# First stage of a conditioned decoder layer: modulation columns in two halves, first products block by block

## The chip, the cores and the metric

The kernel runs on one core of one Trainium2 chip. The metric is the device time of one execution in microseconds (us), the median of several; lower is better. Columns of a matmul are counted along its moving operand; a bank is one of the eight 128 x 512 float32 pieces of PSUM.

## The reference

`x` is (1, 1024, 1024) float32, `c` is (1, 1024). The stage that the change touches computes this (cut to it):

```python
mod = silu(c) @ w_ada + b_ada                  # w_ada: (1024, 6*1024)
sh1, sc1, gt1, sh2, sc2, gt2 = split(mod, 6)
h = rmsnorm(x, norm1_g) * (1 + sc1) + sh1      # (1024, 1024)
proj = h @ w_in                                # (1024, 3600): gq, gk, gv, gg, ga, hq, hf, hi, hg
a_logit = ga @ gla_w_a2 + gla_b_a              # ga has rank 16
```

Behind it come six units of chunked gated linear attention (two GLA pairs of heads, four HGRN2 heads), the output projection with its gated residual, a second modulated norm, a mixture of 32 experts with routing to two of them, and a final modulated norm.

## The kernel before

All work is laid out by hand: five engines, each with its own written order, tied by semaphores. The names in the order and trace rows are those of tiles, and a line of a helper serves all its callers.

**The first stage.** `h` is needed transposed (model dimension on partitions, tokens along the free dimension), as eight inner blocks k of 128 by 1024 tokens, and split in a high part `HT` and a low part `HL` (`HFULL` is the unrounded value and lies at the address of `HL`), since each float32 product is made of three float32r matmuls (`product`, L1945 to L1947: high x high, low x high, high x low). Its steps are:

- SP (the DMA queue of SyncE) loads tokens 0 to 511 of x (two DMAs of 1 MB), then sixteen slices of `w_ada` into `AST`, 512 KB each (eight for the scale `sc1`, eight for the shift `sh1`), then the first of the four weight chunks `WF`, the other half of x, and the other chunks. A chunk is 128 columns of `w_in`, 512 KB.
- ScalarE (ACT) squares x to sums (`square`, L808), takes the root and scales the rows (L815); VectorE does the inverse (`inverse`) and scales the second half's rows (L1288).
- VectorE accumulates `acc += slice * c_act[k]` for sixteen slices of 1024 columns (`add_slice`, L1242 and L1244) into `ACC` (scale) and `ACCB` (shift).
- TensorE (PE) transposes x block by block (`x_transposes`, L1929, four 128 x 128 transposes per block and token half), and sums each accumulator over partitions by `col_job` (L1910): eight matmuls with one moving column, whose stationary operand is 128 columns of the accumulator. Between the two jobs stand two matmuls whose result nobody reads (L1936). VectorE turns the sums into the columns `GS1` and `SH1` (`column`, L1258, L1260).
- Per block, ACT evacuates the transposes with scale and bias to `HT` (`x_evac`, L841), and VectorE makes the low part in two steps (`x_low`, L1320 from PSUM, then L1324).
- TensorE then runs `k_jobs(0)`, one job after the other and each over all eight blocks: query and key of token half 0, the rank-16 gate `ga`, query, key and gate of half 1, then `a`. The blocks of half 1 are transposed between these jobs.

**What follows.** VectorE's order goes on behind the last `x_low` with the small constants, the low parts of the value chunks (`low`, L1309, behind ACT's L822), eight slices for the next row (`unit_slice`, L1242 and L1244, out of the two buffers `AR`, which GpSimd (POOL) refills each time one has been used), and then the decay steps of unit 0 (L1390 onward), on which ACT's exponentials (L850) and the evacuation of value job 1 (L908) wait. TensorE goes on with the value jobs (`gv`), the row job and the jobs of unit 1.

Of the kernel before, what the change touches and what calls it, by code (L numbers as in the profile page):

```python
# [27 lines left out]
F32 = mybir.dt.float32  # L28
# [20 lines left out]
def layer_kernel(nc, x, c, w_ada, b_ada, norm1_g, w_in, gla_w_a2, gla_b_a, gla_norm_g, hg_norm_g,  # L49
# [113 lines left out]
    X_BANK = [2, 3, 4, 5, 6, 1, 2, 3, 4, 5, 6, 7, 2, 3, 4, 5]  # L163
    X_AHEAD = 6
# [28 lines left out]
    with ExitStack() as ctx:  # L193
# [38 lines left out]
        AST = at("AST", 96, [P, 8, D])  # L232
# [153 lines left out]
        COL = [PS[:, b * HALF:b * HALF + KD] for b in (7, 0)]  # L386
# [28 lines left out]
        c_in = sem("c_in")  # L415
# [11 lines left out]
        slab_in = [sem(f"slab_in{i}") for i in range(8)]  # L427
        ar_in = [sem(f"ar_in{i}") for i in range(2)]
        ar_used = sem("ar_used")
        ast_used = sem("ast_used")  # L430
        w_raw = [sem(f"w_raw{i}") for i in range(WSLOTS)]
# [17 lines left out]
        rr_h = sem("rr_h")  # L449
# [4 lines left out]
        xt_done = sem("xt_done")  # L454
# [67 lines left out]
        yg_in = [sem(f"yg_in{t}") for t in range(NT)]  # L522
# [8 lines left out]
        win = w_in.rearrange("a (p k) n -> p (a k) n", k=KD)  # L531
# [3 lines left out]
        def ada_slice(v, k):  # L535
            src, col = ADA[v]
            return ada_w[src][:, k, col:col + D]
# [8 lines left out]
        def _(sp):  # L546
# [3 lines left out]
            def load_early(v):  # L550
                for k in range(KD):
                    n = EARLY.index(v) * KD + k
                    if n >= 8:
                        sp.wait_ge(ast_used, n - 7)
                    sp.dma_start(AST[:, n % 8, :], ada_slice(v, k)).then_inc(slab_in[n % 8], 16)

# [6 lines left out]
            load_early("sc1")  # L563
            load_early("sh1")
            load_chunk(0)
            for g in range(2, NT // 2):
                load_x(g)
            for n in range(1, WSLOTS):
                load_chunk(n)
            last_use = {}  # L570
            for u in range(UNITS):
                for name in ("q", "k", "f"):
                    if (u, name) in chunk_at:
                        last_use[chunk_at[(u, name)]] = number[(u, name, 1)]
# [73 lines left out]
            for t in range(NT):  # L648
                sp.dma_start(YG[t][:, :, :], ys_rows[:, 0:3:2, t, :]).then_inc(yg_in[t], 16)
# [8 lines left out]
        def _(pool):  # L658
# [11 lines left out]
            pool.wait_ge(ast_used, KD + 4)  # L670
            with nc.allow_non_contiguous_dma(reason="short vectors"):
# [9 lines left out]
                pool.dma_start(GCOL[:, 2, :], norm_f_g.rearrange("(p k) -> p k", k=KD)).then_inc(later_in, 16)  # L681
            n = 0
# [105 lines left out]
        def _(act):  # L788
            A = nc.scalar.activation
            act.dma_start(C8[:], col_view(c)).then_inc(c_in, 16)  # L790
            act.wait_ge(c_in, 16)
# [1560 lines left out]
```

## Time and profile before

| | |
|---|---|
| median of 3 runs | 1070.38 us (1068.85 to 1071.96) |
| the profiled execution | 1076.19 us, span 1074.4 us |
| TensorE busy | 991.8 us (92%) |
| VectorE busy | 797.4 us (74%) |
| ScalarE busy | 527.6 us (49%) |
| granted TensorE clock, mean | 0.969 |

The profile is one execution, 0.5% above the median of the runs; its span is 1.8 us shorter than its own time. Busy shares are means over stages with different limits. What happens in the first 110 us is read from the timeline, the chain of waits and the stretches between two instants.

### The profile page before, as it was taken

The numbers are of one execution on the slowest core, as the hardware profiler recorded it, in microseconds if no ns is written. First come the engines' busy times: TensorE is split into PE (matmuls) and PEld (weight loads), VectorE is DVE, ScalarE is ACT, GpSimd is POOL, SyncE is SP. The second block draws the span as 40 slices with busy tenths as digits, with TensorE's granted clock in tenths as the row PEclk, the third lists the DMA queues.
The fourth block names the chain that finished last, engine by engine and source line by source line (L and its number), as shares of the span: only waits on it lengthen the run. The fifth ranks groups of instructions, "written<-read, shape, count | busy, mean of one in ns | idle before, by whom it ended". The sixth has DMA issues, their size and how long they took to land.

```text
span 1074.4 us, 15416 instructions
## 1 busy us (share of the span) xinstructions
PE 991.8 (92%) x5654; PEld 780.0 (73%) x5654; DVE 797.4 (74%) x1476; ACT 527.6 (49%) x921; POOL 118.7 (11%) x151
## 2 busy tenths in 40 slices
PE   2899988999898999999989899789999999999996
PEld 3669778987896998989978688456666666666642
DVE  7768668944992886958677755868888887878828
ACT  4454332653265465555562321265666666565532
POOL 0200001000100000000010000023122112222200
PEclk9798989999998999999989899999999999999998
DMA  9733433330323224130292122789999999999285
GB/s 363 231 98 98 137 99 99 99 98 23 116 80 99 79 76 141 60 99 1 83 402 51 79 80 101 286 295 341 370 374 372 361 366 367 350 353 359 96 304 212
DMA packets 79881, 206.78 MB, mean 192 GB/s; under 512 B 11750, under 2 KB 40502, under 8 KB 71628
## 3 DMA queue, kind: packets, MB, share of 16 engines
q1 hardware_dynamic: 58080, 156.25, 40.2%
q0 software_dynamic: 15120, 43.72, 12.5%
q10 hardware_dynamic: 6620, 6.00, 1.8%
q8 instruction: 39, 0.64, 0.3%
q14 instruction: 22, 0.18, 0.1%
HBM read 189.61 MB, written 24.71 MB: 199 GB/s over the span
## 4 chain that ended last, share of the span: by engine, by line
PE 56%; DVE 22%; DMA 13%; issue 4%; ACT 4%; SPq 0%; ACTq 0%; DVEq 0%; POOLq 0%
PE PS L1945 10%; PE PS L1947 10%; PE PS L1946 10%; DMA WGU<-in_w_exp_up 7%; PE PS L2216 4%; PE PS L2010 3%; DMA AR<-in_w_ada 3%; DVE ACC L1244 3%; DVE AT L1418 3%; PE PS L2224 3%; PE PS L2222 3%; PE PS L2223 3%; DVE WL L1309 2%; PE PS L2207 2%; PE PS L2326 1%
## 5 line engine op out<-in xcount | busy, mean ns | idle before, releaser
L1945 PE MATMUL PS<-WH,HT 128*128 128x256 f32 x512 | 148.9, 291 | 3.9 <-ACT GVB L908 2.2
L1946 PE MATMUL PS<-WL,HT 128*128 128x256 f32 x512 | 146.8, 287 | 0.0
L1947 PE MATMUL PS<-WH,HL 128*128 128x256 f32 x512 | 146.8, 287 | 0.0
L1782 DVE TENSOR_TENSOR WGL<-WGU,WGH 128x1024 fp32r<-128x1024 f32 x96 | 116.9, 1219 | 20.0 <-ACT WGH L1152 18.8
L1418 DVE COPY_PREDICATED AT<-MASK,PS 128x64 f32<-128x64 uint8 x320 | 72.9, 228 | 68.7 <-PE PS L2021 50.2
L1152 ACT ACTIVATE WGH<-WGU 128x1024 fp32r<-128x1024 f32 x96 | 98.6, 1062 | 43.6 <-DMA WGU<-in_w_exp_up 32.6
L1945 PEld LDWEIGHTS PS<-WH,HT 128*128 128x128 f32 x512 | 100.4, 196 | 7.0 <-issue 7.0
L1946 PEld LDWEIGHTS PS<-WL,HT 128*128 128x128 f32 x512 | 100.2, 196 | 0.0
L1947 PEld LDWEIGHTS PS<-WH,HL 128*128 128x128 f32 x512 | 100.2, 196 | 0.0
L2222 PE MATMUL PS<-WGH,XGTH 128*96 128x512 f32 x192 | 88.6, 461 | 0.0
L1820 DVE TENSOR_TENSOR WDL<-WDN,WDH 128x2048 fp32r<-128x2048 f32 x32 | 73.4, 2292 | 16.8 <-ACT WDH L1162 16.8
L1945 PE MATMUL PS<-HT,WH 128*128 128x512 f32 x192 | 79.7, 415 | 3.3 <-DVE HL L1324 2.5
L1000 ACT ACTIVATE O<-PS 128x128 f32<-128x128 f32 x64 | 17.5, 274 | 125.6 <-PE PS L2059 97.7
L1947 PE MATMUL PS<-HT,WL 128*128 128x512 f32 x192 | 76.6, 399 | 0.0
L1946 PE MATMUL PS<-HL,WH 128*128 128x512 f32 x192 | 76.5, 398 | 0.0
L2224 PE MATMUL PS<-WGH,XGTL 128*96 128x512 f32 x192 | 76.0, 396 | 0.0
L2223 PE MATMUL PS<-WGL,XGTH 128*96 128x512 f32 x192 | 75.3, 392 | 0.0
L1244 DVE SCALAR_TENSOR_TENSOR ACC<-AR,CA,ACC 128x1024 f32<-128x1024 f32 x42 | 53.9, 1284 | 27.8 <-DMA AR<-in_w_ada 18.3
L730 POOL DMA_INDIRECT XG<-xn_rows,IDXG x32 | 38.7, 1209 | 307.3 <-DVE YB L1795 112.9
L2216 PE MATMUL PS<-WGU,XGTF 128*96 128x512 f32 x128 | 61.7, 605 | 0.0
L1162 ACT ACTIVATE WDH<-WDN 128x2048 fp32r<-128x2048 f32 x32 | 61.3, 1917 | 0.0
L1140 ACT ACTIVATE XGTH<-PS 128x384 fp32r<-128x384 f32 x32 | 15.7, 490 | 78.9 <-PE PS L2207 78.9
(347 smaller groups left out, 2268.6 us busy)
## 6 DMA issues: line engine op xcount, KB each, us to landing
WGU<-in_w_exp_gate SPq DMA_DIRECT2D x32, 1024.0 KB, 12.4
WGU<-in_w_exp_up SPq DMA_DIRECT2D x32, 1024.0 KB, 18.4
WDN<-in_w_exp_down SPq DMA_DIRECT2D x32, 1024.0 KB, 13.8
AR<-in_w_ada POOLq DMA_DIRECT2D x32, 512.0 KB, 4.0
WF<-in_w_in SPq DMA_DIRECT2D x28, 512.0 KB, 5.6
AST<-in_w_ada SPq DMA_DIRECT2D x16, 512.0 KB, 8.7
AR<-in_w_ada_final POOLq DMA_DIRECT2D x16, 512.0 KB, 4.7
YG<-expert_rows SPq DMA_DIRECT2D x8, 1024.0 KB, 12.5
```

Source lines behind the costliest of these rows:

```text
L1152: A(WGH[(NCH * s + part) % 4][:], WGU[s][:, :, KC * part:KC * part + KC, :], ACT.Copy).then_inc(wgh_ready, 1)
L1244: i = V.scalar_tensor_tensor(out=acc, in0=w, scalar=CA[:, k:k + 1], in1=acc, op0=ALU.mult, op1=ALU.add)
L1418: link(V.copy_predicated(level(a, s)[:, :, 1, :], level(MASK[:, l, :], s)[:, :, 1, :], level(src, s)[:, :, 1, :]))
L1782: V.tensor_tensor(WGL[s][:, :, ks, :], WGU[s][:, :, ks, :], WGH[(NCH * s + c) % 4][:].bitcast(F32), ALU.subtract).then_inc(wgl_ready, 1)
L1820: V.tensor_tensor(WDL[s][:], WDN[s][:], WDH[s % 2][:].bitcast(F32), ALU.subtract)
L1945: MM(ps, wh, xh, start=first, stop=False)
L1946: MM(ps, wh, xl, start=False, stop=False)
L1947: return MM(ps, wl, xh, start=False, stop=last)
L2216: MM(ps, XGTF[:, par, k - KS, :], WGU[s][:, :, k, :], start=(k == KS), stop=False)
L2222: MM(ps, XGTH[:, par, k, :], wh, start=False, stop=False)
L2223: MM(ps, XGTH[:, par, k, :], wl, start=False, stop=False)
L2224: last = MM(ps, XGTL[:, par, k, :], wh, start=False, stop=(k == KS - 1))
```

## The change

All of x is loaded first, and its squares, roots and row scalings are done for both token halves on ACT. The slices of `w_ada` come as column halves of 256 KB (512 columns): part 0 for inner blocks 0 to 3, part 1 for blocks 4 to 7; sixteen slots, 32 slices. The inner dimension is now blocked contiguously (`w_in` as `(k p)`, x as `k * P:(k + 1) * P`), before it was strided (`k::KD`). The bias and gain vectors come in by rows and are transposed on TensorE. Query and key products of unit 0 run block by block into four banks of their own (`FIRST`): four blocks for both token halves, then, behind the sums of part 1, the other four. Four of the shift slices of part 1 are not accumulated on VectorE, but multiplied on TensorE (`shift_slices`). `x_evac` writes both `HT` and `HFULL`, so that `x_low` is one subtraction. Seven unread matmuls take the place of two.

```diff
     def k_jobs(u):
         if is_gla(u):
             if u == 0:
-                return [("q", 0), ("k", 0), ("ga", 0), ("q", 1), ("k", 1), ("ga", 1), ("a", 0), ("a", 1)]
+                return [("ga", 0), ("ga", 1), ("a", 0), ("a", 1)]
...
-    X_BANK = [2, 3, 4, 5, 6, 1, 2, 3, 4, 5, 6, 7, 2, 3, 4, 5]
-    X_AHEAD = 6
+    PARTS = 2
+    KP = KD // PARTS
+    x_order = [(g, k) for part in range(PARTS) for g in range(2) for k in range(KP * part, KP * part + KP)]
+    X_BANK = [4, 5, 6, 7] + [(4, 5, 6)[i % 3] for i in range(12)]
+    early_order = [(v, part, k) for part in range(PARTS) for k in range(KD) for v in range(2)]
+    AST_SLOTS = 16
+    SHIFT_ON_PE = [(1, 1, k) for k in range(KD // 2, KD)]
+    early_on_dve = [e for e in early_order if e not in SHIFT_ON_PE]
+    first_products = [("q", 0), ("k", 0), ("q", 1), ("k", 1)]
...
-            load_early("sc1")
-            load_early("sh1")
-            load_chunk(0)
             for g in range(2, NT // 2):
                 load_x(g)
-            for n in range(1, WSLOTS):
+            load_early(0)
+            load_chunk(0)
+            load_chunk(1)
+            load_early(1)
+            for n in range(2, WSLOTS):
                 load_chunk(n)
...
+            def x_evac(i):
+                g, k = x_order[i]
+                act.wait_ge(xb_ready, i + 1)
+                gs, dst = GS1[:, k:k + 1], slice(g * HALF, (g + 1) * HALF)
+                A(HT[:, k, dst], XB[i], ACT.Identity, scale=gs, bias=SH1[:, k:k + 1])
+                A(HFULL[:, k, dst], XB[i], ACT.Identity, scale=gs, bias=SH1[:, k:k + 1]).then_inc(xh_ready, 1)
...
+            act.wait_ge(mod1_ready, 1)
+            for i in range(8):
+                x_evac(i)
...
+            act.wait_ge(mod1_ready, 2)
+            for i in range(8, 14):
+                x_evac(i)
+            first_evac("q", 0)
+            x_evac(14)
+            first_evac("k", 0)
+            x_evac(15)
...
             scale_rows(0)
+            early_slices(0, 6)
             scale_rows(1)
+            early_slices(6, 16)
+            bias_columns()
+            columns(0)
+            lows(0, k_chunks(0))
+            for i in range(8):
+                x_low(i)
+                early_slices(16 + i, 17 + i)
+            early_slices(24, len(early_on_dve))
+            columns(1)
+            for i in range(8, 16):
+                x_low(i)
...
+            def shift_slices():
+                for i, e in enumerate(SHIFT_ON_PE):
+                    n = early_order.index(e)
+                    pe.wait_ge(slab_in[n % AST_SLOTS], 16 * (n // AST_SLOTS + 1))
+                    for b in range(KP):
+                        last = MM(SUM_SH[1][:, b, 1 + i:2 + i], AST[:, n % AST_SLOTS, b * P:(b + 1) * P], CA[:, e[2]:e[2] + 1],
+                                  start=True, stop=True)
+                last.then_inc(shift_ready, 1)
...
+            for i in range(4):
+                x_transposes(i)
+            pe.wait_ge(small_in, 64)
+            TR(BIAS, BROW[:, :], IDENT[0:3 * KD, 0:3 * KD]).then_inc(col_ready, 1)
+            unread(4)
+            early_sums(0)
+            unread(3)
+            for i in range(8):
+                first_block(i)
+                if i != 3:
+                    x_transposes(i + 4 if i < 3 else i + 3)
+            pe.wait_ge(ca_ready, 1)
+            shift_slices()
+            early_sums(1)
+            for i in range(8, 16):
+                first_block(i)
+                if i + 3 < 16:
+                    x_transposes(i + 3)
+            for name, half in k_jobs(0):
                 k_job(0, name, half)
```

The order that results on TensorE, from its first instruction to the second block of products (`PS<-XR,IDENT` are the unread matmuls, `PS<-ONESF,ACC` the sums over partitions). Before:

```order
L1929 MATMUL PS<-IDENT,XR 128x128 x24
L1910 MATMUL PS<-ONESF,ACC 128x1 x8
L1936 MATMUL PS<-XR,IDENT 128x512 x2
L1910 MATMUL PS<-ONESF,ACCB 128x1 x8
L1945 MATMUL PS<-HT,WH 128x512
L1946 MATMUL PS<-HL,WH 128x512
L1947 MATMUL PS<-HT,WL 128x512
```

With the change:

```order
L1971 MATMUL PS<-IDENT,XR 128x128 x16
L2109 MATMUL PS<-IDENT,BROW 128x24
L1956 MATMUL PS<-XR,IDENT 128x512 x4
L1942 MATMUL PS<-ONESF,ACC 128x1 x4
L1942 MATMUL PS<-ONESF,ACCB 128x1 x4
L1956 MATMUL PS<-XR,IDENT 128x512 x3
L1991 MATMUL PS<-HT,WH 128x512
L1992 MATMUL PS<-HL,WH 128x512
L1993 MATMUL PS<-HT,WL 128x512
```

Ahead of the first product eight transposes and eight sums less are issued, and five unread matmuls and one small transpose more.

TensorE between the eighth and the ninth block of products, with the change (the last rows of block 7, the transposes of block 10, the shift slices, the sums of part 1, the first rows of block 8):

```order
L1991 MATMUL PS<-HT,WH 128x512
L1992 MATMUL PS<-HL,WH 128x512
L1993 MATMUL PS<-HT,WL 128x512
L1971 MATMUL PS<-IDENT,XR 128x128 x4
L1950 MATMUL PS<-CA,AST 128x1 x16
L1942 MATMUL PS<-ONESF,ACC 128x1 x4
L1942 MATMUL PS<-ONESF,ACCB 128x1 x4
L1991 MATMUL PS<-HT,WH 128x512
L1992 MATMUL PS<-HL,WH 128x512
L1993 MATMUL PS<-HT,WL 128x512
```

Before, nothing of this stood between products: twenty-four matmuls of one moving column now do.

VectorE from the first column sums to the second block. Before:

```order
L1258 TENSOR_TENSOR GS_134<-PS,BCOL 128x8
L1260 SCALAR_TENSOR_TENSOR GS_134<-GS_134,GCOL 128x8
L1309 TENSOR_TENSOR WL<-WF,WH 128x1024
L1258 TENSOR_TENSOR SH_135<-PS,BCOL 128x8
L1320 SCALAR_TENSOR_TENSOR HFULL<-PS,GS_134,HT 128x512
L1324 TENSOR_SCALAR HL<-HFULL,SH_135 128x512
L1320 SCALAR_TENSOR_TENSOR HFULL<-PS,GS_134,HT 128x512
L1324 TENSOR_SCALAR HL<-HFULL,SH_135 128x512
```

With the change:

```order
L1280 COPY BCOL<-PS 128x16
L1281 COPY GCOL<-PS 128x8
L1287 TENSOR_TENSOR GS_135<-PS,BCOL 128x4
L1288 SCALAR_TENSOR_TENSOR GS_135<-GS_135,GCOL 128x4
L1290 TENSOR_TENSOR SH_136<-PS,BCOL 128x4
L1344 TENSOR_TENSOR WL<-WF,WH 128x1024 x2
L1354 TENSOR_TENSOR HL<-HFULL,HT 128x512
L1264 TENSOR_SCALAR ACC<-AST,CA 128x512
L1354 TENSOR_TENSOR HL<-HFULL,HT 128x512
L1264 TENSOR_SCALAR ACCB<-AST,CA 128x512
```

Both low parts of the query and key weights now stand ahead of the first low part of x, and behind each of the first eight low parts stands one half slice of part 1.

## Rows read from the trace of the kernel before

**Rows 1.** the page: busy us of each engine, share of the span, instructions

```profile
PE 991.8 (92%) x5654; PEld 780.0 (73%) x5654; DVE 797.4 (74%) x1476; ACT 527.6 (49%) x921; POOL 118.7 (11%) x151
```

**Rows 2.** chain of waits, 60 to 103 us: start us, us, what

```profile
64.78 0.49 DVE HL L1324
...
69.52 0.68 DVE ACC L1242
...
71.80 5.87 DMA AR<-in_w_ada
...
88.35 1.30 DVE ACC L1244
...
101.88 0.36 PE PS L1945
```

**Rows 3.** timeline of PE: start us, us, line, out<-in, instructions [idle before <-releaser]

```profile
18.82 5.36 PE L1929 MATMUL PS<-IDENT,XR 128*128 128x128 f32 x24 [18.82 <-ACT XR L815]
23.97 3.78 PE L1910 MATMUL PS<-ONESF,ACC 128*128 128x1 f32 x16
27.61 3.58 PE L1936 MATMUL PS<-XR,IDENT 128*128 128x512 f32 x4
32.39 3.96 PE L1910 MATMUL PS<-ONESF,ACCB 128*128 128x1 f32 x16 [1.20 <-DVE ACCB L1244]
38.88 0.77 PE L1945 MATMUL PS<-HT,WH 128*128 128x512 f32 x1 [2.52 <-DVE HL L1324]
...
54.15 2.96 PE L1929 MATMUL PS<-IDENT,XR 128*128 128x128 f32 x24 [0.17 <-DVE XR L1288]
...
61.46 0.48 PE L1945 MATMUL PS<-HT,WH 128*128 128x512 f32 x1
...
72.45 0.39 PE L1970 MATMUL PS<-HT,WGS 128*32 128x512 f32 x1
```

**Rows 4.** stretches: from:to, us, busy us (instructions) by engine, granted clock, DMA share, GB/s

```profile
10.00:20.00 10.00, 1.18 (x6) 1.21 (x7) 9.29 (x14) 7.12 (x10) 0.00 (x0) 1.00 1.04 396
...
27.60:31.20 3.60, 3.59 (x5) 1.17 (x5) 3.49 (x4) 0.00 (x0) 3.60 (x6) 0.54 1.10 353
...
38.90:44.50 5.60, 5.60 (x17) 4.66 (x18) 5.42 (x10) 3.62 (x6) 0.00 (x0) 0.50 1.11 334
```

**Rows 5.** timeline of ACT, 5 to 40 us

```profile
6.17 1.06 ACT L808 ACTIVATE SQX<-XR 128x1024 f32<-128x1024 f32 x1 [2.08 <-DMA XR<-in_x]
...
7.36 1.06 ACT L808 ACTIVATE SQX<-XR 128x1024 f32<-128x1024 f32 x1
...
8.85 1.06 ACT L808 ACTIVATE SQX<-XR 128x1024 f32<-128x1024 f32 x1 [0.35 <-DMA XR<-in_x]
...
12.73 0.20 ACT L804 ACTIVATE RR<-TA 128x4 f32<-128x4 f32 x1
14.41 4.27 ACT L815 ACTIVATE XR<-XR,RR 128x1024 f32<-128x1024 f32 x4 [1.47 <-DVE RR L1233]
31.63 1.06 ACT L822 ACTIVATE WH<-WF 128x1024 fp32r<-128x1024 f32 x1 [12.95 <-DMA WF<-in_w_in]
36.65 4.12 ACT L841 ACTIVATE HT<-PS,SH,GS 128x512 fp32r<-128x512 f32 x6 [3.96 <-DVEq L1335]
```

**Rows 6.** timeline of PE, warm unread matmuls at the end of the program

```profile
1023.03 6.17 PE L2308 MATMUL PS<-X,IDENT 128*128 128x512 f32 x14
```

**Rows 7.** timeline of DVE: slices, a column step, a weight chunk's low part

```profile
23.13 9.21 DVE L1244 SCALAR_TENSOR_TENSOR ACCB<-AST,CA,ACCB 128x1024 f32<-128x1024 f32 x7
32.37 0.17 DVE L1258 TENSOR_TENSOR GS<-PS,BCOL 128x8 f32<-128x8 f32 x1
...
32.88 1.23 DVE L1309 TENSOR_TENSOR WL<-WF,WH 128x1024 fp32r<-128x1024 f32 x1
```

**Rows 8.** line L1320 alone: instructions, ns min/median/max, first and last start

```profile
L1320 DVE SCALAR_TENSOR_TENSOR HFULL<-PS,GS,HT x16: 744/746/751, 37.5 to 64.0; 128x512 f32<-128x512 f32 x16
```

**Rows 9.** timeline of PE: transposes whose stationary columns are adjacent, at full clock

```profile
220.26 1.23 PE L2046 MATMUL PS<-IDENT,O 128*128 128x128 f32 x8 [0.25 <-ACT GVB L908]
```

More of the change, by code:

```diff
@@ L426, in layer_kernel @@
         br_in = sem("br_in")
-        slab_in = [sem(f"slab_in{i}") for i in range(8)]
+        slab_in = [sem(f"slab_in{i}") for i in range(AST_SLOTS)]
         ar_in = [sem(f"ar_in{i}") for i in range(2)]
@@ L548, in load_x, with load_early @@
                 sp.dma_start(XR[:, 2 * g:2 * g + 2, :], x_rows[:, 2 * g:2 * g + 2, :]).then_inc(x_in[g], 16)
[L550 to L555, printed above, removed]
+            def load_early(part):
+                for n, (v, p, k) in enumerate(early_order):
+                    if p == part:
+                        if n >= AST_SLOTS:
+                            sp.wait_ge(ast_used, n - AST_SLOTS + 1)
+                        sp.dma_start(AST[:, n % AST_SLOTS, :], ada_slice(EARLY[v], k, part * HALF, HALF)).then_inc(
+                            slab_in[n % AST_SLOTS], 16)
             def load_chunk(n):
@@ L808, in square @@
                 chain(A(SQX[:], XR[:, t, :], ACT.Square, accum_out=SS[:, t:t + 1]))
-            for t in range(4):
-                square(t)
-            root_of(0, 4, D).then_inc(rr_ready, 1)
-            act.wait_ge(inv_ready, 1)
-            for t in range(4):
-                A(XR[:, t, :], XR[:, t, :], ACT.Copy, scale=RR[:, t:t + 1]).then_inc(xr_ready, 1)
+            for g in range(2):
+                for t in range(4 * g, 4 * g + 4):
+                    square(t)
+                root_of(4 * g, 4 * g + 4, D).then_inc(rr_ready, 1)
+            for g in range(2):
+                act.wait_ge(inv_ready, g + 1)
+                for t in range(4 * g, 4 * g + 4):
+                    A(XR[:, t, :], XR[:, t, :], ACT.Copy, scale=RR[:, t:t + 1]).then_inc(xr_ready, 1)
             act.wait_ge(table_zero, 16)
@@ L826, in highs @@
                     high(u, name)
-            high(0, "q")
+            highs(0, k_chunks(0))
             def evac(job):
@@ L833, in evac, with first_evac @@
                 return pj_free[n % 2]
[L835 to L842 removed]
+            def x_evac(i):
[4 more added lines that the diff above has]
+                A(HFULL[:, k, dst], XB[i], ACT.Identity, scale=gs, bias=SH1[:, k:k + 1]).then_inc(xh_ready, 1)
+            def first_evac(name, half):
+                n = first_products.index((name, half))
+                act.wait_ge(first_ready, n + 1)
+                A((Q if name == "q" else K)[:, 0, half * HALF:(half + 1) * HALF], FIRST[(name, half)], ACT.Copy,
+                  scale=float(P // 2) ** -0.5 if name == "q" else 1.0).then_inc(first_free, 1)
             def item(u, i):
@@ L959, in _ @@
             highs(0, v_chunks(0))
-            for name, half in k_jobs(0)[3:]:
+            first_evac("q", 1)
+            first_evac("k", 1)
+            for name, half in k_jobs(0):
                 k_evac(0, name, half)
@@ L1964, in k_job @@
                 for k in range(KD):
-                    if (u, name) == (0, "q"):
-                        pe.wait_ge(xl_ready, half * KD + k + 1)
-                        if half == 0 and k == 2:
-                            x_transposes(0, range(X_AHEAD, KD))
                     if name == "ga":
```

177 lines of the change are left out of this document (81 added, 96 removed).

## Prediction

> **What bounds the kernel now.** The page says that TensorE is busy 92% of the span and VectorE 74% [rows 1]; that is an average, so I went on to the first 110 us. The chain of waits there [rows 2] is the view that decides: it does not run over TensorE, but from the last low part of x (VectorE, L1324, ends at 65.3 us) through the value weights to eight slices out of `AR`, of which the chain waits for the transfers (69.5 to 89.65 us), through the decay steps to the value job that starts at 101.88. So the number to forecast is when the last low part of x is ready: what it slips, everything behind it slips, since the eight slices stand behind it in VectorE's order. The timeline of TensorE [rows 3] shows the stage before it: transposes from 18.8, first product at 38.88, then nearly unbroken work. The stretches [rows 4] give the clock: 0.50 of full speed (the 1.2 GHz level) for the first 5.6 us of products, because the column sums and an idle time lay ahead of them.
>
> **How rows and instructions go together.** The written order has eight column sums where the trace has sixteen rows [rows 3], and two unread matmuls where it has four: a plain float32 matmul stands in two rows. So one column sum costs 3.78 / 8 = 0.47 us, and the second job of eight took 3.96 us, 0.49 each, with the clock partly down: its price hardly hangs on the clock. A transpose is one row.
>
> **The change, step by step.**
>
> 1. *x first.* The two MB of x landed for squares at 6.17 and 8.85 [rows 5]; at 396 GB/s [rows 4] each further MB takes 2.6 us, so the other half is there at 11.5 and 14.1 and is not waited for. A square costs 7.36 - 6.17 = 1.19 [rows 5]: four more from 12.93 end at 17.7, the root at 18.1. Four row scalings take 4.27 [rows 5], so the first transposes start at 22.4, not 18.8. The later four scalings end at 26.7, ahead of the two weight chunks. The sixteen half slices (4.2 MB) land by 24.7. The first weight chunk was there at 31.63, behind 10.5 MB [rows 5]; now the second one ends 9.4 MB, so by about 30, and ACT's two high parts (1.06 each) end by 32 and are not late.
> 2. *VectorE, part 0.* A slice of 1024 columns costs 9.21 / 7 = 1.32 [rows 7]; I take half, 0.66, for 512 columns (upper bound 0.75, a 512-column operation of this kind from PSUM [rows 8]). Sixteen and the two inverses end at 26.6. TensorE is later than that, so VectorE is not the bound.
> 3. *TensorE up to the sums.* 16 transposes at 5.36 / 24 = 0.22 [rows 3] end at 26.0, the bias transpose at 26.2. Four unread matmuls: two took 3.58 [rows 3], 1.79 each at the low clock; fourteen rows took 6.17 [rows 6], 0.88 per matmul at full clock. Before, the clock came back 2.9 us into this work (mean 0.54 over 3.6 us, rows 4). So 1.6 of them at 1.79 and 2.4 at 0.88: 5.0 us, to 31.2 (bounds 29.7 and 33.4). Eight sums, 3.8: 35.0.
> 4. *To the first product.* Three column steps on VectorE at 0.2 [rows 7]: 35.6. ACT now evacuates twice, 4.12 / 6 = 0.69 each [rows 5]: 37.0. VectorE makes two weight low parts first (1.23 each, rows 7): 38.1; then one subtraction of 512 columns, half of 1.23: 38.7. First product at 38.9, where it was 38.88. Nothing is gained up to here. The three unread matmuls (2.6) lie in this wait and should keep the clock up, so I take full speed for what follows.
> 5. *Blocks 0 to 7.* 48 rows from 61.46 to 72.45 [rows 3]: 0.229 per matmul. 48 matmuls 11.0, plus 28 transposes at 2.96 / 24 = 0.123 [rows 3], 3.4: to 53.3. ACT needs 1.4 per block, VectorE 0.6 + 0.66; both keep up, and VectorE's last half slice (28th) is done at about 53.
> 6. *The stop in the middle.* Sixteen shift matmuls and eight sums, all of the form of the column sum: 24 x 0.47 = 11.3 us, to 64.6. No product can cover them, since block 8 needs what they give, and the transposes that could run ahead (three banks) have run. Before, the same eight sums of the scale lay ahead of the first product, where TensorE had nothing to do. Moving four half slices saves VectorE 4 x 0.66 = 2.6 us and costs TensorE 7.6. Then four column steps 0.8, two evacuations 1.4, a subtraction 0.6: block 8 starts at 67.4.
> 7. *Blocks 8 to 15.* The clock falls in those 14 us, as it did before behind far less; the low stretch then lasts 5.6 us [rows 4] and costs half of it, 2.8. The last x transposes stand behind block 12: 30 matmuls 6.9, 20 transposes 2.5, clock 2.8: 79.6. ACT, held up by two evacuations of finished products (0.6 each), is done with block 15 at 81.3, the last low part at 81.9. Before: 65.3. **The slip is 16.6 us.**
> 8. *Behind it.* Constants, value weights and the eight slices are the same instructions: 24.4 us from the last low part to the end of the slices [rows 2], transfers of 0.5 MB through two buffers. That they are hidden better or worse I bound by 2 us either way: 5.87 was waited in the longest case [rows 2], where two weight chunks were loading too; these now wait for the first gate job, and so fall into the slices again. TensorE is through its gate jobs at 81.9 + (6 + 32) x 0.229 = 90.6, before at 72.45 + 16 x 0.229 = 76.1 [rows 3]: 14.5 later, less than VectorE's slip, so it doesn't set more.
> 9. *At nothing.* New loads of bias rows (landed long before TensorE has done its transposes), merged semaphores, the two evacuations where ACT was idle.
>
> **Rules against rows.** The rows of the column sums stand 3.78 / 16 = 0.236 us apart [rows 3], and the sum goes by that. The Trainium skill (TensorE: Matmul & The Clock Gate, LDWEIGHTS) gives a weight load of 128 columns 107 ns; an estimate by it makes the thirty-two small matmuls cost 3.4 us, not 15.1, and the whole change +5 us.
> With adjacent stationary columns, at full clock, eight transposes took 1.23, 0.15 each with the tail [rows 9]; with columns eight apart 0.123 [rows 3]. The Trainium skill (SBUF — State Buffer, Door 1) says that accesses which cross to a new 16-byte line pay a penalty, which would speak for this change's contiguous blocks; these two rows show none.
>
> **The sum.** Made on the profiled execution: 1076.2 + 16.6 = 1092.8. That execution stands 0.5% above the median; on the median: 1070.4 + 16.6 = 1087.0.
>
> **Rivals.**
> - *The clock stays down.* If the three unread matmuls don't hold it, they take 5.4 instead of 2.6 (first product 1.7 later) and blocks 0 to 7 pay 2.8: +21, 1091.5. For it: the column sums that stand between the two unread groups lost the clock before. Against: the second group ends about 1 us ahead of the products.
> - *The small matmuls are cheap.* If each takes the pace of a transpose, 0.123 [rows 3], the thirty-two save 32 x 0.35 = 11.2: +5.4, 1075.8. For it: the one moving column is next to nothing, and a transpose loads as many stationary columns. Against: 0.47 in both jobs. The page on TensorE comes to about this time.
> - *Other side: strided reads were the cost.* All stationary operands of the sums and transposes were read eight elements apart, now they are adjacent. If that brings a small matmul to 0.12 (part 0 ends 2.8 earlier, the stop shrinks from 11.3 to 2.9) and 48 transposes to half price (2.9), and the clock outlives the short stop (2.8): 16.6 - 2.8 - 8.4 - 2.9 - 2.8 = -0.3, and 1070. From 0.12 a small matmul down it is no loss, below that a gain, to about 1067. Against it: rows 9. The page on SBUF has this rule.
> - *The change does not reach the end:* the slip is taken up behind the stage. TensorE waits little there and VectorE's chain has only transfers to give: 2 us, not 16. I see no more, but a chain is one view.
>
> **How the numbers follow.** Forecast 0.64, clock down 0.12, cheap small matmuls 0.12, other side 0.07, taken up behind 0.05. A difference under 0.3% (3.2 us) can't be told from none with this kernel. Slower: 0.64 + 0.12 + 0.12 = 0.88; the last two cases, 0.12, are half same (0.06), half faster (0.06). The forecast's own range is 1082 to 1091 (step 3's bounds, the transfers, the runs' 1.5 us). With the clock case above and the cheap one below it becomes 1075 to 1093.
>
> **What would show it.** In the changed profile: first product within 2 us of 38.9; the shift matmuls as 32 rows at 0.236 each and 16 rows of sums behind them, with no product between; clock 0.50 in the stop and for some 5 us of block 8 and on; the last `HL` at 80 to 84 us; the value job's start at about 118. Wrong if the stop is shorter than 6 us, if the first product stands before 35, or if the last `HL` slips but the value job does not.

## The result, and the profile after

The changed kernel takes 1080.75 us (median of 4 runs, 1078.54 to 1083.05) against 1069.66 for the kernel before, run beside it on the same chip (1068.85 to 1071.96): ratio 1.010, 95% interval 1.0072 to 1.0128. That is slower by 11.1 us, where 16.6 was forecast (1087.0, range 1075 to 1093). The profiled execution took 1083.05 us, with a span of 1081.2 and a mean granted clock of 0.969, as before.

On the page after, TensorE is busy 995.1 us and VectorE 787.2, before 991.8 and 797.4 [rows 1]; nothing can be read from that. The timeline of TensorE up to the second part's first product is the counterpart of [rows 3]:

```profile
22.18 3.65 PE L1971 MATMUL PS<-IDENT,XR 128*128 128x128 f32 x16 [22.18 <-ACT XR L831]
25.76 0.30 PE L2109 MATMUL PS<-IDENT,BROW 24*128 24x24 f32 x1
25.99 4.16 PE L1956 MATMUL PS<-XR,IDENT 128*128 128x512 f32 x8
29.98 0.95 PE L1942 MATMUL PS<-ONESF,ACC 128*128 128x1 f32 x8
30.79 1.03 PE L1942 MATMUL PS<-ONESF,ACCB 128*128 128x1 f32 x8
31.69 2.82 PE L1956 MATMUL PS<-XR,IDENT 128*128 128x512 f32 x6
35.64 0.50 PE L1991 MATMUL PS<-HT,WH 128*128 128x512 f32 x1 [1.13 <-DVE HL L1354]
...
49.90 3.63 PE L1950 MATMUL PS<-CA,AST 128*128 128x1 f32 x32
53.40 1.07 PE L1942 MATMUL PS<-ONESF,ACC 128*128 128x1 f32 x8
54.33 1.84 PE L1942 MATMUL PS<-ONESF,ACCB 128*128 128x1 f32 x8
59.36 0.79 PE L1991 MATMUL PS<-HT,WH 128*128 128x512 f32 x1 [3.19 <-DVE HL L1354]
```

The first product stands at 35.64, 3.2 us earlier than the 38.88 of before, and the stop in the middle is there, as 32 rows (the shift matmuls) and 16 rows (the sums), but it lasts 9.5 us from its first row to block 8, not 14.1. The stretches after (before, and the meaning of the columns: [rows 4]) show the clock: up through blocks 0 to 7, at 0.50 (1.2 GHz) from 54.3 to 64.5, the end of the stop and the first five us of block 8 and on.

```profile
36.00:50.00 14.00, 14.00 (x78) 11.64 (x76) 11.56 (x18) 7.92 (x13) 1.06 (x2) 1.00 0.71 212
50.00:54.30 4.30, 4.30 (x41) 4.30 (x40) 0.67 (x1) 0.00 (x0) 0.00 (x0) 0.99 0.53 208
54.30:64.50 10.20, 7.01 (x24) 5.95 (x24) 2.74 (x7) 5.44 (x8) 0.00 (x0) 0.50 0.00 0
```

The chain of waits after, behind the last low part of x (before: [rows 2]):

```profile
72.64 0.69 DVE HL L1354
...
80.07 7.17 DMA AR<-in_w_ada
...
99.02 1.29 DVE ACC L1266
...
112.55 0.55 PE PS L1991
```

The last low part ends at 73.3, before at 65.3: 8.1 us. The eight slices end at 100.3, before at 89.65: 10.7. The value job starts at 112.55, before at 101.88: 10.67 us. So 8.1 us are lost ahead of that low part and 2.6 behind it. That these 10.7 reach the end rests on the medians, which differ by 11.1. The two traces agree with it only in part: the last head output (`OTS`) is evacuated 9.3 us later (538.4 against 529.1), but the spans differ by 6.8. Of the difference 3.5 us stand in one place, where the first gather of the experts' rows waits 8.0 us behind the last store of `XN` in the trace of before and 4.5 in the one after; over all the traces of this case that wait lies between 4.4 and 8.1, and none of the edits touches it.

### The profile page after: what moved, and what is told of

It is laid out like the page before. It is cut to its first block, busy times and chain, and to the rows that moved or that the text cites. A ratio compares the mean times of both kernels' runs of the same rounds, so it can differ in the third digit from the quotient of the medians.

```text
span 1081.2 us, 15575 instructions
## 1 busy us (share of the span) xinstructions
PE 995.1 (92%) x5697; PEld 781.7 (72%) x5697; DVE 787.2 (73%) x1474; ACT 542.0 (50%) x941; POOL 108.5 (10%) x151
## 4 chain that ended last, share of the span: by engine, by line
PE 60%; DVE 19%; DMA 11%; ACT 5%; issue 4%; ACTq 0%; SPq 0%; DVEq 0%; POOLq 0%
PE PS L1991 11%; PE PS L1993 10%; PE PS L1992 10%; DMA WGU<-in_w_exp_up 7%; PE PS L2272 4%; PE PS L2053 3%; PE PS L2280 3%; PE PS L2278 3%; PE PS L2279 3%; DVE AT L1448 3%; DMA AR<-in_w_ada 3%; DVE ACC L1266 2%; DVE WL L1344 2%; PE PS L2263 1%; PE PS L2382 1%
## 5 line engine op out<-in xcount | busy, mean ns | idle before, releaser
L1991 PEld LDWEIGHTS PS<-WH,HT 128*128 128x128 f32 x512 | 100.4, 196 | 11.3 <-issue 11.3
L1992 PEld LDWEIGHTS PS<-WL,HT 128*128 128x128 f32 x512 | 100.3, 196 | 0.0
```

Source lines behind the costliest of these rows:

```text
L1991: MM(ps, wh, xh, start=first, stop=False)
L1992: MM(ps, wh, xl, start=False, stop=False)
```

## The experiments

Each run has beside it runs of the kernel before on the same chip; ratios are to those. Each was traced once. "FD" is VectorE's step behind the eight slices (100.34 us in the changed kernel), the last landmark of the stage that stands in all of these kernels.

**Stride put back.** The sums and shift matmuls read their stationary columns four elements apart; the sums then belong to other columns of the model dimension than the rest of the kernel takes them for, and nothing else differs.

```diff
-   last = MM(dst, acc[:, lo:lo + P], ONESF[:, 0:1], ...)
+   last = MM(dst, acc[:, part * HALF + b:(part + 1) * HALF:KP], ONESF[:, 0:1], ...)
...
-   ... AST[:, n % AST_SLOTS, b * P:(b + 1) * P], CA[:, e[2]:e[2] + 1],
+   ... AST[:, n % AST_SLOTS, b::KP], CA[:, e[2]:e[2] + 1],
```

> The changed kernel, but the stationary columns of its column sums and shift matmuls lie four elements apart (the sums then belong to other columns; nothing else is altered). In the changed kernel such a matmul took 0.22 us (two rows 0.108 apart) where I had forecast 0.47 from the kernel before. Theory A (the clock made the difference): they still take 0.22 at full clock, the 24 in the middle about 6 us, last HL at 73 us, time as the changed kernel, 1081. Theory B (adjacent columns made it): 0.4 to 0.47 each, the middle 10 to 11 us, first product 1 to 2 us later, last HL at 78 to 81, time 1086 to 1088.

One run, 1083.91 us (before on that chip: 1069.95). Timeline of TensorE, this experiment:

```profile
29.84 1.80 PE L1942 MATMUL PS<-ONESF,ACC 128*128 128x1 f32 x8
31.49 2.00 PE L1942 MATMUL PS<-ONESF,ACCB 128*128 128x1 f32 x8
...
51.88 7.52 PE L1950 MATMUL PS<-CA,AST 128*128 128x1 f32 x32
59.27 2.00 PE L1942 MATMUL PS<-ONESF,ACC 128*128 128x1 f32 x8
61.13 2.00 PE L1942 MATMUL PS<-ONESF,ACCB 128*128 128x1 f32 x8
66.33 0.79 PE L1991 MATMUL PS<-HT,WH 128*128 128x512 f32 x1 [3.19 <-DVE HL L1354]
```

The same instructions at the same places take twice as long: 32 shift rows 7.5 us and not 3.6, the first two groups of sums 1.65 and 1.87 us from start to start and not 0.81 and 0.90. The stop is 14.5 us, and with it the forecast's stop comes out nearly to the number (14.1). The first two groups are the clean comparison, since the granted clock is 1.00 there in both kernels; in the stop it fell at 54.0, among the shift rows, and they kept their distance of 0.23 us. Two stretches of this experiment:

```profile
30.00:32.00 2.00, 2.00 (x11) 2.00 (x10) 0.00 (x0) 0.00 (x0) 1.69 (x3) 1.00 1.13 279
...
56.00:58.00 2.00, 2.00 (x10) 2.00 (x10) 0.00 (x0) 0.00 (x0) 0.00 (x0) 0.50 0.00 0
```

The weight loads of these rows (line of the first group's sums alone: ns min/median/max), first this experiment, then the changed kernel:

```profile
L1942 PEld LDWEIGHTS PS<-ONESF,ACC x16: 307/329/329, 29.4 to 60.9; 128*128 128x128 f32 x16
```

```profile
L1942 PEld LDWEIGHTS PS<-ONESF,ACC x16: 190/192/232, 29.6 to 54.1; 128*128 128x128 f32 x16
```

What follows: the price of a small matmul is set by how its stationary columns are read, 0.41 to 0.47 us when they are strided and 0.22 when adjacent, at full clock. That is theory B. The last low part starts at 79.4 (72.6 in the changed kernel) and the landmark `FD` at 106.1, 5.8 us later. The one time, 1083.9, is only 3.2 above the changed kernel's median and below theory B's 1086 to 1088. The 6.6 us by which the first head output is late in this trace (236.1 against 229.5) are 5.1 at the last one, so I take the size from the landmarks of the stage.

**Contiguous blocks in the kernel before.** Only the layout and the bias rows, nothing split.

```diff
-   win = w_in.rearrange("a (p k) n -> p (a k) n", k=KD)
+   win = w_in.rearrange("a (k p) n -> p (a k) n", p=P)
...
-   last = MM(ps[:, k:k + 1], acc[:, k::KD], ONESF[:, 0:1], ...)
+   last = MM(ps[:, k:k + 1], acc[:, k * P:(k + 1) * P], ONESF[:, 0:1], ...)
...
-   last = TR(XB[i][:, t * P:(t + 1) * P], XR[:, 4 * g + t, k::KD], IDENT[:])
+   last = TR(XB[i][:, t * P:(t + 1) * P], XR[:, 4 * g + t, k * P:(k + 1) * P], IDENT[:])
```

> The kernel before, with nothing of the change but the contiguous inner blocks (w_in, x and accumulators by k * P:(k + 1) * P, bias and gain by rows and one small transpose). Theory A (stride costs nothing, the clock does all): sums as before, 3.96 us, 1069.7 as before. Theory B (stride costs half of a small matmul): the second job of eight sums 1.8 to 2.2 us instead of 3.96, first product at 36.7 to 37.1, then the same 5.6 us at half clock, time 1067.5.

1070.3 us against 1069.95, ratio 1.000 (0.9983 to 1.0017). Its TensorE timeline:

```profile
25.42 1.95 PE L1916 MATMUL PS<-ONESF,ACC 128*128 128x1 f32 x16
27.23 1.96 PE L1944 MATMUL PS<-XR,IDENT 128*128 128x512 f32 x4
33.53 3.57 PE L1916 MATMUL PS<-ONESF,ACCB 128*128 128x1 f32 x16 [4.33 <-DVE ACCB L1247]
39.62 0.76 PE L1953 MATMUL PS<-HT,WH 128*128 128x512 f32 x1 [2.53 <-DVE HL L1327]
```

The first job fell from 3.78 [rows 3] to 1.95: theory B as to the price. The second did not, and the rest of theory B missed: TensorE, done sooner, then waited 4.33 us for VectorE, the clock went to 0.50, and sixteen rows took 3.57 us at 1.2 GHz. So adjacent columns cost 0.11 us a row at the upper level and 0.21 at the lower; strided ones cost 0.21 to 0.24 at either (last experiment ahead of block 0 and in its stop, and [rows 3]). A faster engine waited longer, lost its clock and gave the gain back.

A second thing hides in this comparison. The whole stage starts later here: `c` landed about 1.2 us later, VectorE's first row is at 5.28 and not at 4.12, and its last early slice ends 1.1 us later. So the first product at 39.62 against 38.88 is 0.4 us early if counted from VectorE's start. In all twelve other traces that row is at 5.06 to 5.59; of the kernel before there is one trace, so whether the other layout of the small loads does this, or that one execution was early, is open.

**The same with three unread matmuls behind the second job.**

```diff
    col_job("sh1", ACCB, ast_used, 2 * KD)
+   pe.wait_ge(mod1_ready, 1)
+   for _ in range(3):
+       MM(PS[:, 7 * HALF:8 * HALF], IDENT[:], XR[:, 0, 0:HALF], start=True, stop=True)
```

> As b_contig, and three unread matmuls behind the second job of column sums (2.6 us at full clock, inside the wait for the first low part). Theory A (the clock is held as in the changed kernel): the first products at full clock, first product at 37, the 2.8 us of the half-speed stretch gone as well, time 1064.5 to 1065.5. Theory B (the clock falls anyway, or the unread ones delay the first product): as b_contig or slower by up to 2.

1070.94 us, ratio 1.0003 (0.9985 to 1.002). Theory B. The clock had fallen before the second job, and work behind it comes too late:

```profile
33.49 3.57 PE L1916 MATMUL PS<-ONESF,ACCB 128*128 128x1 f32 x16 [3.88 <-DVE ACCB L1247]
36.92 5.30 PE L1948 MATMUL PS<-XR,IDENT 128*128 128x512 f32 x6
41.40 1.05 PE L1956 MATMUL PS<-HT,WH 128*128 128x512 f32 x1
```

**Nothing of the shift on TensorE** (the changed kernel, VectorE makes those four half slices itself).

```diff
-   SHIFT_ON_PE = [(1, 1, k) for k in range(KD // 2, KD)]
+   SHIFT_ON_PE = []
```

> The changed kernel, but all four shift slices are accumulated on VectorE (SHIFT_ON_PE empty). TensorE loses 32 rows (3.5 us) in the middle; VectorE's last half slice ends at 50.7 + 4 x 0.78 = 53.8 instead of 50.7, and TensorE waits for it from 49.9. Theory A (the stop is set by TensorE's small matmuls): sums 2 us at full clock, stop 2 us or more shorter, 1079. Theory B (the stop is a chain over three engines, and what TensorE sheds VectorE takes on): sums end at 53.8 + 2.7 = 56.5 against 56.2, time within 1 us of 1081.

1077.9 us, ratio 1.0061 (1.0042 to 1.0081). TensorE in the stop:

```profile
53.56 1.02 PE L1940 MATMUL PS<-ONESF,ACC 128*128 128x1 f32 x8 [3.12 <-DVE ACC L1266]
...
59.17 0.79 PE L1988 MATMUL PS<-HT,WH 128*128 128x512 f32 x1 [2.98 <-DVE HL L1352]
```

The 3.5 us that TensorE sheds it waits for VectorE; block 8 is where it was (59.17 against 59.36), `FD` at 99.35. The sums end at 56.2, which is theory B. The median is 2.9 us lower than the changed kernel's (by the ratios, 1.0061 against 1.010, it is about 4), of which the landmarks show 1.0. In the traces another 2.6 lie between the first and the last head output: 306.3 us here, 308.9 in the changed kernel. That stretch holds the same work in all kernels and takes 306.1 to 309.1 over all the traces, so I don't count it to the edit.

**The split taken back** (all slices, shift matmuls and both groups of sums ahead of block 0).

```diff
    early_sums(0)
-   unread(3)
-   ...
    pe.wait_ge(ca_ready, 1)
    shift_slices()
    early_sums(1)
+   unread(3)
+   for i in range(8):
+       first_block(i)
...
-   early_slices(6, 16)
+   early_slices(6, len(early_on_dve))
```

> The changed kernel with the split taken back: VectorE makes all slices before the first product, the shift matmuls and both groups of sums stand ahead of block 0, and the sixteen blocks follow without a stop. VectorE's part-0 slices end at 28.0 us in the changed kernel and twelve more at 0.785 us would end at 37.5; then 48 small rows at 0.11 (about 5 us, or twice that at the low clock), and the first product at 42 to 45, 7 to 9 us later than the changed kernel's 35.64. Theory A (the stop costs what TensorE stands without products in it, 9.5 us from 49.9 to 59.36, and the low clock behind it some 2.5 us more, so the split gives back more than it won): the last low part of x at 68 to 71 instead of 73.3, and 1075 to 1079. Theory B (the total work ahead of block 15 is the same and only its place changes): last low part within 1 us of 73.3, and 1080 to 1082. If it comes out over 1083, the split was worth having.

1084.11 us, ratio 1.0132 (1.011 to 1.0154): over 1083, so neither theory, and the third case. Its TensorE:

```profile
38.12 6.96 PE L1946 MATMUL PS<-CA,AST 128*128 128x1 f32 x32 [7.00 <-DMA AST<-in_w_ada]
44.94 1.84 PE L1938 MATMUL PS<-ONESF,ACC 128*128 128x1 f32 x8
46.65 1.84 PE L1938 MATMUL PS<-ONESF,ACCB 128*128 128x1 f32 x8
48.35 4.85 PE L1952 MATMUL PS<-XR,IDENT 128*128 128x512 f32 x6
53.64 0.50 PE L1987 MATMUL PS<-HT,WH 128*128 128x512 f32 x1 [0.43 <-DVE HL L1354]
```

I had priced VectorE's slices (end of the last: 37.5 expected, 42.2 measured) and not the slabs' transfers: TensorE waits 7.0 us for a slab, and does the next 14 us of work at the lower level. The first product is at 53.6, the last low part ends at 79.4. With x first and half slices, the split does gain something (`FD` at 100.3, here 105.1), so it is the frame around it that loses. Which part of the frame (x first, the half slices, the second evacuation, products block by block) loses how much, no run separates.

**The two late weight chunks earlier.**

```diff
-   sp.wait_ge(pj_ready, last_use[before] + 1)
+   if before < 2:
+       sp.wait_ge(first_ready, 4)
+   else:
+       sp.wait_ge(pj_ready, last_use[before] + 1)
```

> The changed kernel, where SyncE waits for four of the first product's blocks instead of the first gate job ahead of the two late weight chunks (their slots are free by then), so these 2.1 MB move before the eight slices of VectorE and not beside them. The changed kernel's slices took 22.6 us from their first row to the decay steps (77.70 to 100.3), the kernel before 20.2, with 7.17 and 5.87 us of waiting for one transfer. Theory A (the chunks beside the slices cost them their transfers): 20 us or less for the slices and 1077.5 to 1079. Theory B (the slices are bound by their own 4.2 MB through two buffers, whatever moves beside them): 22 to 23 us and 1080 to 1082.

1077.1 us, ratio 1.0064 (1.0041 to 1.0087). VectorE's timeline, the first slice and the step behind the eighth, this experiment and then the changed kernel:

```profile
77.64 0.75 DVE L1267 TENSOR_SCALAR ACC<-AR,CA 128x1024 f32<-128x1024 f32 x1
...
97.00 1.23 DVE L1423 TENSOR_TENSOR FD<-FD,GVB 128x1024 f32<-128x1024 f32 x1
```

```profile
77.70 0.75 DVE L1264 TENSOR_SCALAR ACC<-AR,CA 128x1024 f32<-128x1024 f32 x1
...
100.34 1.22 DVE L1420 TENSOR_TENSOR FD<-FD,GVB 128x1024 f32<-128x1024 f32 x1
```

19.4 us for the slices, not 22.6: theory A. The median moved by 3.7. Two things are to be set right in what I had expected. The two chunks are 1.05 MB together, not 2.1. And the semaphore counts finished products and not blocks, so they are issued at 75.2 and not at 79.0, 2.4 us ahead of the first slice where they were 1.3 behind it; that was enough to get them mostly out of the way.

The size is less certain than the two rows make it look. With the chunks issued behind the first slice the eight slices took 21.0 to 22.6 us (six traces, mean 21.6), with both issued ahead of it 19.4 here and 21.0 in the three mends below. In the kernel before, where one goes ahead and one falls among them, they took 20.2. So the chunks cost up to 3.3 us, about 1.4 on the mean.

**Two unread matmuls fewer** (`unread(4)` becomes `unread(2)` ahead of the first sums).

> The changed kernel with two unread matmuls ahead of the first sums instead of four. VectorE's half slices end at 28.03 us, the sums start at 29.98 behind the unread ones. Theory A (the unread ones only delay the sums, 0.88 us each at full clock, once the clock is up): sums at 28.2, first product at 33.9 instead of 35.64, the stop 1.7 earlier, and 1078.5 to 1079.5. Theory B (with fewer of them the clock falls again ahead of the first product): a first product at 34 to 35 at the low clock, 2.8 us lost behind it, and 1080.5 to 1082.

1078.27 us, ratio 1.0078 (1.0054 to 1.0102). TensorE:

```profile
33.97 0.50 PE L1991 MATMUL PS<-HT,WH 128*128 128x512 f32 x1 [1.13 <-DVE HL L1354]
...
48.24 4.55 PE L1950 MATMUL PS<-CA,AST 128*128 128x1 f32 x32
52.65 1.84 PE L1942 MATMUL PS<-ONESF,ACC 128*128 128x1 f32 x8
...
59.40 0.79 PE L1991 MATMUL PS<-HT,WH 128*128 128x512 f32 x1 [3.19 <-DVE HL L1354]
```

The first product is 1.7 us earlier, as theory A has it, at full clock. But in this stop the clock is at 0.50 from 50.7 us on, behind some 23 of the 32 shift rows, where the changed kernel kept it until the second group of sums: rows that took 0.11 us take 0.21, and block 8 starts at 59.40 as before. The 1.7 us are gone in the stop. `FD` is at 98.68, 1.7 earlier, by slices that took 21.0 us; the last low part ends at 73.3 as before, so that gain is not the one expected.

**One unread matmul in the stop.**

```diff
    shift_slices()
+   for _ in range(2):
+       MM(PS[:, 7 * HALF + 256:8 * HALF], IDENT[:], XR[:, 0, 0:256], start=True, stop=True)
    early_sums(1)
```

> The changed kernel with one unread matmul (two of 256 columns) between the sixteen shift matmuls and the sums of the second part. In the changed kernel the clock fell at about 54.3 us, 4.4 us after the last product, and stayed at 0.50 until 64.5. Theory A (a matmul of full width in the stop keeps the clock): it costs 0.9 to 1 us of TensorE, the second job of sums stays at 1.03 us instead of 1.84, and blocks 8 to 10 run at full clock (2.5 us less): the last low part of x at 70.5 to 72 instead of 73.3, and 1078.5 to 1080. Theory B (it only delays, and the clock falls all the same): block 8 at 60.3 instead of 59.36, low clock until 65, and 1081 to 1082.5.

1081.09 us, ratio 1.011 (1.0088 to 1.0132): theory B. Its stretches:

```profile
50.00:55.00 5.00, 5.00 (x44) 4.90 (x42) 0.99 (x2) 0.00 (x0) 0.00 (x0) 0.99 0.50 193
55.00:66.00 11.00, 7.81 (x29) 6.81 (x30) 2.74 (x7) 5.23 (x8) 0.00 (x0) 0.54 0.00 0
```

The clock went down behind it all the same, at 54.9, and block 8 came at 61.07, 1.7 later; 0.35 of that stood ahead of the stop already (first shift row at 50.25 against 49.90).

**Three mends together** (two unread, no shift on TensorE, the chunks early).

> The changed kernel with three mends at once: two unread matmuls instead of four ahead of the first sums, no slices moved to TensorE, and the two late weight chunks loaded early. Alone they brought 2.5, 2.9 and 3.7 us against the changed kernel's 1080.75. Theory A (they are worth on different stretches, so they add up): 1071.5 to 1073. Theory B (first and second both end in the stop, where VectorE's slices or the clock take the gain): 1074 to 1076. In neither is it under the kernel before: the stop of TensorE in the middle stays.

1075.8 us, ratio 1.0065 (1.0044 to 1.0086): theory B, at its upper end. By ratio three mends together can't be told from the best of them alone (1.0064). In the trace the last low part ends at 71.0 (2.3 earlier, where each of the first two alone moved it by nothing: one had VectorE behind it, the other the clock) and `FD` stands at 96.4, 3.9 earlier.

**The kernel before, adjacent columns, clock held.** Six unread matmuls between the two groups of sums instead of two, and two behind them.

```diff
-   for _ in range(2):
+   for _ in range(6):
        MM(PJ[0], IDENT[:], XR[:, 0, 0:HALF], start=True, stop=True)
    col_job("sh1", ACCB, ast_used, 2 * KD)
+   pe.wait_ge(mod1_ready, 2)
+   for _ in range(2):
+       MM(PJ[0], IDENT[:], XR[:, 0, 0:HALF], start=True, stop=True)
```

> The kernel before with inner blocks in rows of their own (adjacent stationary columns, as in the changed kernel), without split, and six unread matmuls instead of two between the two groups of sums, two more between the second group and the first product. So TensorE works until about 33.2, when VectorE has the second matrix ready (33.5). Theory A (the clock is all that kept the adjacent columns from a gain): the second group of sums at full clock takes 1.9 us instead of 3.6, first product at 38.0 instead of 38.9, the first blocks at full clock (2.8 us), last low part of x at 61.5 instead of 65.3, and 1065.5 to 1068. Theory B (behind the first product VectorE and ScalarE set the pace, 16 low parts at 1.3 us and more, or the clock falls in any case): last low part at 64 to 66, and 1069 to 1071.

1068.89 us, ratio 0.9993 (0.9983 to 1.0004): theory B. TensorE:

```profile
27.06 7.09 PE L1944 MATMUL PS<-XR,IDENT 128*128 128x512 f32 x12
33.99 1.84 PE L1916 MATMUL PS<-ONESF,ACCB 128*128 128x1 f32 x16
...
38.36 0.47 PE L1956 MATMUL PS<-HT,WH 128*128 128x512 f32 x1 [0.23 <-DVE HL L1327]
39.45 0.50 PE L1956 MATMUL PS<-HT,WH 128*128 128x512 f32 x1 [0.16 <-DVE HL L1327]
```

The second job at the upper level takes 1.84, and the stretch 38.9 to 44.5 has a granted clock of 1.00 where it had 0.50 [rows 4]. Yet each of the first blocks of products now waits for VectorE's low part, and these come 1.18 us apart in both kernels. The last one ends at 64.5, before at 65.3. The 2.8 us that I had put on the clock in this stage weren't there to win.

**And VectorE relieved.** In that kernel ScalarE makes the whole value of inner blocks 2, 4 and 6, and squares two rows of x earlier.

```diff
+   FULL_ON_ACT = (2, 4, 6)
...
+   if k in FULL_ON_ACT:
+       last = A(HFULL[:, k, dst], XB[i], ACT.Identity, scale=GS1[:, k:k + 1], bias=SH1[:, k:k + 1])
...
+   if k in FULL_ON_ACT:
+       v_.sem_inc(xt_done, 1)
+       V.tensor_tensor(HL[:, k, hs], HFULL[:, k, hs], HT[:, k, hs].bitcast(F32), ALU.subtract)...
+       continue
```

> The kernel before with adjacent columns and the held clock (as in b_hold), in which VectorE set the pace of the first blocks at 1.18 us per low part. Here ScalarE makes the whole value of three of eight inner blocks, as the changed kernel does for all (VectorE then needs one subtraction of about 0.65 us), and squares two of the later four rows of x ahead of its last evacuations. Theory A (the stage before was bound by VectorE at 1.18 us a block, and by ScalarE's squares ahead of the second half of x): the second group of transposes at 51 to 52 us instead of 53.45, the last low part of x at 60.5 to 62 instead of 64.0 (64.8 in the kernel before), and 1065 to 1067. Theory B (ScalarE is then the bound, or TensorE's products are): last low part at 63 to 65, and 1068 to 1070.

1066.35 us against 1068.62, ratio 0.9979 (0.9963 to 0.9996), the only one of these kernels that is below the kernel before, by 0.2%. VectorE:

```profile
61.23 0.69 DVE L1332 TENSOR_TENSOR HL<-HFULL,HT 128x512 fp32r<-128x512 f32 x1 [1.06 <-ACT HFULL L849]
...
62.62 0.49 DVE L1338 TENSOR_SCALAR HL<-HFULL,SH 128x512 fp32r<-128x512 f32 x1
```

The last low part starts at 62.6, 2.2 us earlier than the 64.78 of [rows 2]; ScalarE is late at block 6 and gives a part of it back. The landmark lies between the two theories, and the time is in theory A's range.

## Why the prediction was right, and where its sum was wrong

The sign, the place and the shape held: the number to forecast was the last low part of x, TensorE stood without products in the middle, the clock fell there, and what was lost up to the low part went through to the end. The size didn't. Of the 16.6 us 8.1 came, and 2.6 more came from behind.

Of the signs that I had named, the numbers missed: the first product was to be within 2 us of 38.9 (35.64), the small rows 0.236 apart (0.11), the last low part at 80 to 84 (73.3), the value job at about 118 (112.55). The order of the rows, the clock in the stop and behind it, and the value job slipping with the low part held. The time is below the forecast's own range (1082 to 1091) and within the wide one only through the lower bound that I had drawn for cheap small matmuls. And it is closer to the forecast than the working deserves: 2.6 us behind the low part, which the sum had at nothing, made up for a third of what was priced too high ahead of it.

- *Step 1, x first.* Transposes from 22.18 (forecast 22.4), done at 25.76 with the bias transpose behind them. Right.
- *Step 2, VectorE.* The half slices stand 0.785 us apart, 16.04 to 16.82: worse than the upper bound I gave (0.75), and 0.66 was my value. Half the columns cost 0.6 of the time. It did no harm, since TensorE's sums came later; it would in the version without a split.
- *Step 3, up to the sums, failed twice.* The four unread matmuls (eight rows) took 4.0 us, not 5.0: only the first row was slow, 0.99 us, the other seven stood 0.43 apart. The reading behind the 5.0 was off too: a mean of 0.54 over 3.6 us [rows 4] leaves 3.3 us at the lower level and not 2.9. And the two groups of sums took 1.7, not 3.8. First product 35.64 instead of 38.9.
- *Step 4.* From the sums to the product 3.9 us forecast, 3.95 measured.
- *Step 5, blocks 0 to 7.* 14.4 forecast, 14.3 measured.
- *Step 6, the stop, failed by its price.* "24 x 0.47 = 11.3 us": it was 6.2 (49.90 to 56.1), of which the shift rows 3.5 at full clock and the sums 2.8, the second job with the clock down. The wait behind it, 2.8 forecast, was 3.2. With 0.22 at the upper level for twenty of them and 0.43 at the lower for four the term would have been right (6.1). The stride experiment gives the old price back, so this step is settled.
- *Step 7.* The clock fell, and stayed down for 5.1 us from block 8 on (5.6 forecast). 14.5 us forecast for the blocks, 14.0 measured, and each of the last low parts waits for ScalarE (1.13 us before the last one), as the step had it.
- *Step 8, behind it.* I gave 2 us either way and took 0; it was +2.6, so the bound was too narrow. The two weight chunks ran beside the slices, which the step named; the early chunks show that they are a cause, and the spread of the traces (above) that their share is up to 3.3 us and not fixed closer.

The terms so put right: 16.6 - 3.3 (step 3) - 4.6 (stop) - 0.6 (the rest) + 2.6 = 10.7.

**Where I misjudged the evidence.** The rule against my price was in the text: the Trainium skill (SBUF — State Buffer, Door 1) has a penalty for accesses that cross to a new 16-byte line, and I set it aside since [rows 9] and [rows 3] show transposes at 0.15 and 0.12 us whether their columns are adjacent or not. That was true of the distance between transposes and no evidence on the small matmuls: 24 transposes take 2.96 us strided and 2.84 adjacent, in the kernel before and in the one with contiguous blocks, while a job of sums takes 3.78 and 1.95. The trace agrees with the rule once one looks at the weight loads of the same 24 transposes (busy us, mean ns), first the kernel before, then contiguous blocks:

```profile
L1929 PEld LDWEIGHTS PS<-IDENT,XR 128*128 128x128 f32 x24 | 2.8, 194 | 0.6 <-DVE XR L1288 0.6
```

```profile
L1935 PEld LDWEIGHTS PS<-IDENT,XR 128*128 128x128 f32 x24 | 2.6, 140 | 0.5 <-DVE XR L1291 0.5
```

The load is longer when strided there too, 194 ns against 140, but a transpose moves 128 columns and the next load runs beside it, so the distance hardly shows it. (That these columns hide it is my reading of the overlap; no run varies them.) The transposes of [rows 9] show their 140 ns in the trace of the kernel before, so both numbers were there to be compared.

The Trainium skill (TensorE: Matmul & The Clock Gate, LDWEIGHTS) was nearer than I took it to be. Its 107 ns for a load of 128 columns is the distance of the adjacent rows at full clock (0.81 us for eight, 0.10 each), though not at the lower level, where they stand 0.21 apart; my estimate by it, 3.4 us for the 32 small matmuls, counted one load for each, where the rows that I had read before showed two. By two it is 6.8, and the 32 took 8.0 us (1.7, 3.5 and 2.8), the last four with the clock down. And the rival of the strided reads I priced too high, since it also took half of the transposes' time and the whole clock with it: at 0.12 a small matmul, where 0.22 came. The truth lay between two of my rivals and the forecast.

One row of before could have told me. I wrote that the price "hardly hangs on the clock" (3.78 and 3.96, [rows 3], the second with the clock partly down) and used it to carry 0.47 over. In these runs the adjacent rows follow the clock (0.11 and 0.21) and the strided ones don't (0.21 to 0.24), so a price on TensorE that stayed the same over both levels was a hint that something other than its clock set it; and the change altered just how the operand is read.

**What stays open.** Why the slices behind the low part took 21.0 to 22.6 us in kernels that had the chunks at the same place, and 19.4 and 21.0 in the two that had them early. Why times and landmarks part by up to 3 us (no shift on TensorE, stride put back): the stretch between the first and the last head output and the wait ahead of the first gather differ by 3.0 and 3.7 us from trace to trace, which is enough to cover it, but with one trace of each kernel it can't be pinned down; the verdicts rest on the landmarks there. And what each part of the frame around the split costs.

## What to carry to other kernels

A price read off one row holds for its access pattern as much as for its shape: where a change alters the stride of an operand, take the old row as a bound and not as the cost, and don't take the distance of another kind of instruction as evidence: compare the weight loads themselves. If a duration doesn't change between the two clock levels, ask what feeds the engine. And before counting on an engine made faster, see what it waits for next: three times here (the second sums at the lower clock, the first products behind VectorE, the stop behind VectorE's slices) the gain became a wait.

## What the runs showed of the hardware

- A float32 matmul with one moving column and 128 stationary ones stands in two rows; with the stationary columns adjacent the rows are 0.11 us apart at full clock and 0.21 at 0.50, with columns four or eight elements apart 0.21 to 0.24 at either. So at the lower level the stride costs next to nothing. Weight loads of the sums at full clock: 192 ns adjacent, 329 strided; at the lower level the adjacent ones take 333.
- Transposes hardly show the stride in their distance, 0.118 against 0.123 us each in a row of 24, but do in their weight loads, 140 against 194 ns.
- The clock fell in the middle of small matmuls that followed each other without a gap: in the changed kernel in the second group of sums (54.3), with an earlier stop among the shift rows (50.7), with strided columns among them too (54.0), and with one unread matmul among them still by the sums (54.9).
- At the start of the program the granted clock is not enough to go by: it reads 1.00 from 18.8 us in the kernel before and from 22.2 in the changed one, yet the first transposes stand 0.22 us apart, strided or adjacent, where later ones stand 0.12, and in the changed kernel the pace doubles only behind the first unread row.
- A `SCALAR_TENSOR_TENSOR` on VectorE takes 0.785 us from start to start on 512 columns and 1.32 on 1024: half the columns cost more than half.
